# The modulation's partition sums as two-row products beside the attention, stored and turned once behind it

## What is computed

```
mod = jnp.dot(jax.nn.silu(cond), w_ada) + b_ada
sh1, sc1, gt1, sh2, sc2, gt2 = [m[:, None, :] for m in jnp.split(mod, 6, axis=-1)]
h = _rmsnorm(x, g_pre_mix) * (1 + sc1) + sh1
z = jnp.einsum('bld,de->ble', h, w_in)
...                                    # mLSTM over chunks in both directions, pooling mixer
x = x + gt1 * _rmsnorm(y, g_post_mix)
h2 = _rmsnorm(x, g_pre_ffn) * (1 + sc2) + sh2
...                                    # convolutional feed-forward
x = x + gt2 * _rmsnorm(f, g_post_ffn)
```

## Time and profile before

| | us |
|---|---|
| median of 3 runs (lowest, highest) | 1732.97 (1732.83, 1733.44) |
| the profiled execution's own time | 1731.54 |
| its span in the trace | 1729.7 |
| busy: PE | 1716.1 |
| busy: DVE | 1265.7 |
| busy: ACT | 703.4 |
| busy: POOL | 256.4 |

### The profile page before, as it was taken

The page is one execution under the profiler, slowest core; times in us unless marked ns, Lnnn a source line. Parts: engine busy times, 40 slices in busy tenths (PEclk is TensorE's granted clock), DMA queues, the critical chain, the costliest instruction groups (busy, mean ns, idle before and its releaser), DMA issues.

```text
span 1729.7 us, 27434 instructions
## 1 busy us (share of the span) xinstructions
PE 1716.1 (99%) x10568; PEld 1621.7 (94%) x10568; DVE 1265.7 (73%) x2754; ACT 703.4 (41%) x1300; POOL 256.4 (15%) x255
## 2 busy tenths in 40 slices
PE   8999999999999999999999999999999999999998
PEld 3999999999999999999988899999999999888887
DVE  4777677677677777573465589888888888788998
ACT  4543222343234243461244454433344334444454
POOL 1010000100100100010000061444333333100000
PEclk9999999999999999999999999999999999999999
DMA  9214333443344455364242331333322222686876
GB/s 347 68 44 148 86 116 113 124 116 124 106 129 148 121 154 169 136 228 147 74 139 91 111 103 66 111 105 104 105 76 67 71 70 69 215 277 218 273 249 245
DMA packets 216279, 236.21 MB, mean 137 GB/s; under 512 B 11568, under 2 KB 160828, under 8 KB 216148
## 3 DMA queue, kind: packets, MB, share of 16 engines
q1 hardware_dynamic: 200916, 179.54, 34.3%
q0 software_dynamic: 10752, 38.00, 6.4%
q10 hardware_dynamic: 4480, 16.91, 2.4%
HBM read 181.49 MB, written 52.92 MB: 136 GB/s over the span
## 4 chain that ended last, share of the span: by engine, by line
PE 93%; DVE 3%; DMA 1%; ACT 1%; SPq 1%; issue 0%; POOL 0%; ACTq 0%; DVEq 0%; POOLq 0%
PE ps L1470 23%; PE ps L1105 13%; PE ps L1107 12%; PE ps L1106 12%; PE ps L1412 6%; PE ps L1487 5%; PE ps L1488 5%; PE ps L1489 5%; PE ps L1277 2%; PE ps L1293 2%; PE ps L1294 1%; PE ps L1295 1%; PE ps L1134 1%; PE ps L1128 1%; DMA adaw<-in_w_ada_dram 1%; PE ps L1220 1%
## 5 line engine op out<-in xcount | busy, mean ns | idle before, releaser
L1105 PE MATMUL ps<-H_hi,ring_hi 128*128 128x384 f32 x1200 | 406.1, 338 | 0.4
L1107 PE MATMUL ps<-H_hi,ring_lo 128*128 128x384 f32 x1200 | 401.8, 335 | 0.0
L1106 PE MATMUL ps<-H_lo,ring_hi 128*128 128x384 f32 x1200 | 401.8, 335 | 0.0
L1105 PEld LDWEIGHTS ps<-H_hi,ring_hi 128*128 128x128 f32 x1200 | 225.6, 188 | 1.9 <-DVE H_lo L2208 1.6
L1106 PEld LDWEIGHTS ps<-H_lo,ring_hi 128*128 128x128 f32 x1200 | 225.6, 188 | 0.2
L1107 PEld LDWEIGHTS ps<-H_hi,ring_lo 128*128 128x128 f32 x1200 | 225.4, 188 | 0.0
L1470 PE MATMUL ps<-T_hi,up_hi 128*128 128x288 f32 x608 | 130.7, 297 | 0.3 <-ACT held_g L2043 0.3
L1470 PE MATMUL ps<-T_lo,up_hi 128*128 128x288 f32 x608 | 130.4, 296 | 0.0
L1470 PE MATMUL ps<-T_hi,up_lo 128*128 128x288 f32 x608 | 130.3, 296 | 0.0
L2208 DVE TENSOR_TENSOR up_lo<-up_raw,up_hi 128x512 fp32r<-128x512 f32 x114 | 88.4, 778 | 57.2 <-ACT up_hi L2001 57.2
L2441 DVE SCALAR_TENSOR_TENSOR ada_part<-raw,condT,ada_part 128x128 f32<-128x128 f32 x448 | 120.3, 346 | 0.0
(11 more groups left out here) (347 smaller groups left out, 3765.9 us busy)
## 6 DMA issues: line engine op xcount, KB each, us to landing
raw<-in_w_in_dram SPq DMA_DIRECT2D x44, 512.0 KB, 4.1
up_raw<-in_w_up_dram SPq DMA_DIRECT2D x38, 512.0 KB, 5.3
w_raw<-in_w_down_dram SPq DMA_DIRECT2D x66, 256.0 KB, 3.3
raw<-in_w_ada_dram SPq DMA_DIRECT2D x32, 512.0 KB, 5.1
X<-z_f SPq DMA_DIRECT2D x44, 256.0 KB, 4.0
GE<-z_gates SPq DMA_DIRECT2D x72, 128.0 KB, 3.8
w_sub<-in_w_down_dram SPq DMA_DIRECT2D x33, 256.0 KB, 3.9
z_w_diff<-w_raw SPq DMA_DIRECT2D x22, 256.0 KB, 2.5
```

Of the source, the lines that this page charges most:

```text
L1105: pe.matmul(out, whi, xhi, start=first, stop=False)
L1106: pe.matmul(out, whi, xlo, start=False, stop=False)
L1107: return pe.matmul(out, wlo, xhi, start=False, stop=last)
```

## The change

The sums 17 to 47 are made in another way and in another place; sum 16 stays as it was.

- DVE: behind the 16 products it copies `ada_part` (both conditionings, 128x256) into a high part, `part_hi`, and writes the rest as `part_lo`, which lies in the same memory as `ada_part`. Both are linked, that is each waits until the instruction before it is done.
- PE: `ada_sum` no longer stands ahead of the unit's blocks, but between block 0 and block 1. It is two matmuls with a stationary operand of two columns of ones (`ones_pair`), moving `part_hi` and then `part_lo` (256 columns), into bank 2. Ahead of it PE waits until bank 2 has been evacuated, and ahead of block 2 until ACT has evacuated block 0.
- ACT: it copies the row of 256 sums to `mod_row` (one partition), evacuates block 0, and issues a DMA of that row to `z_mod` ahead of the exponentials.
- DVE: `mod_row` lies in the memory of `kw_lo`, so ahead of the first kw tile it waits until the row is stored (`mod_rows_stored`). `part_hi` lies in the second half of a tile of `SC` that ACT now fills only by half in step 1.
- Behind the attention POOL loads the 62 rows, PE turns them once (step d == 2), and DVE adds the bias for all of them at once and forms the coefficients in step d == 4 (`second_coef`) instead of ahead of step 0.
- In unit 8 DVE does `pool_group` ahead of the products and no longer behind them.

What is moved and added on PE and on DVE stands in the listings of the order, and of those parts the diff below shows only a line or two.

```diff
+    part_hi = place("part_hi", [P, 2, P], F32R, at=base[0] - 2048 * SEEN + 1024)
     ada_part = place("ada_part", [P, 2, P])
+    part_lo = place("part_lo", [P, 2, P], F32R, at=base[0] - 1024)
+    mod_row = place("mod_row", [1, 2 * P], at=base[0] - 1024)     # behind kw_lo
...
             def ada_sum(a):
                 pe.wait_ge(ada_summed, a - ADA0 + 1)
-                for cond in range(2):
-                    mm = pe.matmul(ps[:, 0, 400 + cond:401 + cond], ada_part[:, cond, :], ones[:, :], start=True, stop=True)
+                if a == ADA0:
+                    for cond in range(2):
+                        mm = pe.matmul(ps[:, 0, 400 + cond:401 + cond], ada_part[:, cond, :], ones[:, :], start=True, stop=True)
+                else:
+                    for n, part in enumerate((part_hi, part_lo)):
+                        mm = pe.matmul(ps[0:2, 2, 0:2 * P], ones_pair[:, :], part[:, :, :].rearrange("p c n -> p (c n)"),
+                                       start=(n == 0), stop=(n == 1))
                 mm.then_inc(ada_used, 1)
...
                 for b in range(NB):
                     take0(q0 + b)
+                    if b == 2 and m > RU and m in ADA_AT:
+                        pe.wait_ge(evac0, q0 + 1)
...
+                    if b == 0 and m > RU and m in ADA_AT:
+                        take0(q0 + 2)
+                        ada_sum(ADA_AT[m])
...
+                if d == 2:
+                    pe.wait_ge(mod_rows_in, 16)
+                    pe.transpose(ps[:, 6, P:P + 2 * ROWS], mod_rows[:, :], ident[0:2 * ROWS, 0:2 * ROWS]).then_inc(rows_turned, 1)
...
+                    else:
+                        if rows_by(m) > 1:
+                            act.wait_ge(mod_rows_stored, 16 * (rows_by(m) - 1))
+                        act.activation(mod_row[:, :], ps[0:1, 2, 0:2 * P], ACT.Copy)
...
+                    if m > RU and m in ADA_AT:
+                        act.wait_ge(evac0, q0 + 1)
+                        act.dma_start(z_mod[rows_by(m) - 1:rows_by(m), :], mod_row[:, :]).then_inc(mod_rows_stored, 16)
...
+                if i < NT - 1 and rows_by(SEG + e):
+                    dve.wait_ge(mod_rows_stored, 16 * rows_by(SEG + e))
...
+                                link(ins)
+                                link(dve.tensor_copy(part_hi[:, :, :], ada_part[:, :, :]))
+                                sub_hi(part_lo[:, :, :], ada_part[:, :, :], part_hi[:, :, :]).then_inc(ada_summed, 1)
```

More of the change, by code:

```diff
@@ L142, in build, with rows_by @@
             ADA_AT[s] = ADA0 + len(ADA_AT)
+    ROWS = 48 - ADA0 - 1
+    def rows_by(m):
+        return sum(1 for s, a in ADA_AT.items() if s <= m and a > ADA0)
     raw_items = []
@@ L398, in build @@
     z_rows = nc.dram_tensor("z_rows", (2, 2, DM), F32, kind="Internal").ap()
+    z_mod = nc.dram_tensor("z_mod", (ROWS, 2 * P), F32, kind="Internal").ap()
     x1_dram = nc.dram_tensor("z_x1", (NT, P, DM), F32, kind="Internal").ap()
@@ L1321, in _ @@
                 take0(q0)
-                if m in ADA_AT:
-                    ada_sum(ADA_AT[m])
+                if m == RU:
+                    ada_sum(ADA0)
                 pe.wait_ge(lo_ready, m + 2 if kind == "v" and idx % 2 == 0 else m + 1)
@@ L1884, in _ @@
                     act.wait_ge(att_weights, seg + 1)
-                    act.activation(SC[:, seg % NT - 1, :, :], ps[:, 3, :].rearrange("p (a b) -> p a b", b=P),
+                    parts = 2 if seg % NT == 1 else 4
+                    act.activation(SC[:, seg % NT - 1, 0:parts, :], ps[:, 3, 0:parts * P].rearrange("p (a b) -> p a b", b=P),
                                    ACT.Copy).then_inc(att_cached, 1)
@@ L2229, in rows @@
                 return vT[:, col:col + n].unsqueeze(2).to_broadcast([P, n, 2])
+            dve.wait_ge(pool_seq, 7)
+            dve.tensor_copy(ones_pair[:, :], ones[:, :].to_broadcast([P, 2]))
             dve.wait_ge(small_in, 16 * 7)
@@ L2443, in ada_products @@
                         if k == KD - 1 and cond:
-                            ins.then_inc(ada_summed, 1)
+                            if a == ADA0:
+                                ins.then_inc(ada_summed, 1)
+                            else:
+                                link(ins)
+                                link(dve.tensor_copy(part_hi[:, :, :], ada_part[:, :, :]))
+                                sub_hi(part_lo[:, :, :], ada_part[:, :, :], part_hi[:, :, :]).then_inc(ada_summed, 1)
                         else:
@@ L2537, in _, with second_coef @@
                         head_scale(NORM_AT[m])
-            dve.wait_ge(evac0, 3 * use_of[("main", NM - 1)] + 3)
-            dve.scalar_tensor_tensor(out=coefA2[:, :, :], in0=modT[:, 32:40, :], scalar=1.0, in1=rows(V_GPF, KD),
-                                     op0=ALU.add, op1=ALU.mult)
-            for n, (mod, gain) in enumerate(((16, V_GQM), (40, V_GQF))):
-                ins = dve.tensor_tensor(coefG[:, n, :, :].rearrange("p c k -> p k c"), modT[:, mod:mod + KD, :], rows(gain, KD), ALU.mult)
-            ins.then_inc(coef2, 1)
+            def second_coef():
+                dve.wait_ge(rows_turned, 2)
+                at = ADA0 + 1
+                link(dve.tensor_tensor(modT[:, at:48, :], ps[:, 6, P:P + 2 * ROWS].rearrange("p (a c) -> p a c", c=2),
+                                       rows(V_BADA + at, ROWS), ALU.add))
+                dve.scalar_tensor_tensor(out=coefA2[:, :, :], in0=modT[:, 32:40, :], scalar=1.0, in1=rows(V_GPF, KD),
+                                         op0=ALU.add, op1=ALU.mult)
+                for n, (mod, gain) in enumerate(((16, V_GQM), (40, V_GQF))):
+                    ins = dve.tensor_tensor(coefG[:, n, :, :].rearrange("p c k -> p k c"), modT[:, mod:mod + KD, :],
+                                            rows(gain, KD), ALU.mult)
+                ins.then_inc(coef2, 1)
             for d in range(KD):
+                if d == 4:
+                    second_coef()
                 k = HEAD_ORDER[d]
```

31 lines of the change are left out of this document (18 added, 13 removed).

## The result

The changed kernel takes 1810.43 us (median of 4 runs, 1806.07 to 1812.34); the kernel before took 1733.2 us beside it (4 runs, 1732.83 to 1734.85). The ratio is 1.0435, 95% interval 1.0423 to 1.0448: slower by 4.35%. The forecast was 1771, range 1756 to 1787. The direction was right and the size was not: the time went up by 77 us where 38 were forecast, and it lies outside the range. The profiled execution of the changed kernel took 1809.66 us with a span of 1807.8 us, 78.1 us longer than the span before.

A forecast was written before the change was run, and what follows sets the result against it. PE was taken to bound the kernel. Unit terms 20.6 + 14.9 + 3.1 + 0.9 - 1.4 = +38.1 us took the profiled 1731.54 to about 1769.7, the median to 1771; range 1756 to 1787.

The forecast's parts named there:

- the 2.0 us of cover: In step 7, head 0, DVE ends v_lo 2.01 us before PE needs it; delay ahead of v_lo is free up to that.
- Sum to products: From the sum's start on PE behind block 0 until DVE can start the next products: 0.44 us.
- The copies: DVE's added copy and subtraction for part_hi and part_lo, with the wait for the last product: 0.76 us, bounds 0.6 to 0.95.
- the restart: PE starting again after waiting for DVE's v_lo, with a slower first matmul: about 0.17 us a stall, bounds 0 to 0.3.
- plain unit: One of 12 units in steps 2 to 7 without turns or gaps: +1.72 us each, 20.6 us in all.
- turn unit: One of 5 units with a sum and one more DVE instruction over 1152 columns: +2.97 us each, 14.9 us.
- covered units: Seven units with a sum where PE would not wait: each gains 0.2 us, -1.4 us in all.
- the smallest transfer listed lands after 3.1 us: Landing time taken for the stored row, so that it is there before DVE reaches kw at 11.9 us into the unit.
- rival 4: PE's clock falls during the new waits; one block at 1.2 GHz after each of 24 stalls, 100 us: 1870. Chance 4%.
- the one stall that I read: PE's idle time of 1.49 us ahead of 46.46 us, where the slice around it still showed the full clock.
- the short bounds: Lower bounds for release, copies and restart: 0.47 us less over 24 stalls, 11 us, giving 1760.
- Rival 3: The row's store lands late, after 7.3 us, so kw waits in 20 units: +20 us, 1791. Chance 8%.

## Why the prediction was wrong, and where it was right

**Right: what bounds the kernel, and the 2.0 us of cover.** PE is the bound, and DVE's idle time behind v_lo gave no cover. The version with the sum 1.0 us into block 0 stays inside the 2.0 and has no stall; the changed kernel, 2.8 us late and with the copies on top, stalls in 24 units, as counted.

**Right: the sizes in a unit.** Block 0 was to be 4.16 and took 4.17. Sum to products was to be 0.44 and took 297.01 - 296.50 = 0.51. The copies were to be 0.76: products to ring_lo now take 301.87 - 297.01 = 4.86 where they took 4.07, so 0.79. From block 0's start to the attention products the forecast said 14.65, and it is 306.98 - 292.33 = 14.65. That the two agree to the hundredth is luck: the sum to the products is 0.07 longer, the copies 0.03 and the block 0.01, while the restart costs 0.05 to this mark and not 0.17. Its slow first matmul falls behind the mark, and adds its 0.1 to the period. The period of a plain unit grew by 1.84 us (forecast 1.72), of a turn unit without a clock fall by 3.2 (2.97), of step 8 by 0.79 (0.69), of step 0 of the last head by 1.18 (1.0), of an odd value unit without the store's wait by 0.29 (0.3). The covered units gained 0.12 and not 0.20. Together 40.3 to 41.8 us where the sum said 38.1. PE's stalls were 1.75 to 1.81 and 3.08 to 3.13 us (1.9 and 3.2).

On the copies, the page "VectorE: DVE Perf Modes" of the Trainium skill (section "The DRAIN you can't avoid") would have taken off 0.10 a sum. The copy starts at 301.20, 0.04 behind the end of the last product (297.40 + 3.76) and some 0.39 behind that product's start, while products come every 0.26: the overlap was lost as forecast. No run here separates what the semaphore itself costs from the overlap that goes with it; the two together cost the 0.1.

**Wrong: "the smallest transfer listed lands after 3.1 us".** This step took the landing of a 64 KB transfer, the smallest that it listed, for all units and made the late landing a rival with a chance of 8%, thought of as 20 units and 7.3 us. It was four units and 7.8 to 10.3 us, worse than the upper bound, because POOL's stores of the state's last column are in the queues there. The other units' rows landed in 1.1 to 3.0 us. The mistake was to take one duration for a transfer without asking, unit by unit, what else is in flight. The stores were in the trace of before, once a head, and smaller than the smallest that the forecast read: 0.5 KB, landing after 10.1 us in the row of before shown with the result. Nor was 7.3 us the slowest kind: loads of 1024 KB took 13.1 us in that trace. A look at the DMA issues beside step 1 would have shown the stores. Price: 15.9 us of stalls where 3 were forecast, 13.1 us, and the clock falls behind the longer stalls.

**Wrong: rival 4's chance and its form.** It was given 4% and the price of "one block at 1.2 GHz behind each of 24 stalls", 100 us. Since the one stall that I read, 1.49 us, kept the full clock, I put the clock at nothing in the sum. The runs show a price between: 9 of 24 stalls are followed by a fall, and a fall takes 1.4 to 3.0 us, 19.8 us in all. The row used as evidence was one execution and a lucky one: the same stall was followed by a fall in six of the twelve traces. It was also shorter than the stalls that were forecast, 1.9 and 3.2 us. One execution of a stall shorter than those it is to bear out bounds nothing. The page "TensorE: Matmul & The Clock Gate" of the Trainium skill (section "HAM oscillation — how this bites in real kernels") was the better witness: by it waits that recur between bursts of work bring the array back to half rate. The traces agree in kind, with a fall behind 33 of 36 stalls of 3.08 us or more; the waits of the page's own example are as long as those or longer, and it gives no price for stalls of 1.8 us, of which 11 of 47 lost the clock. The traces do not show every stall doing so, which the 100 us of the rival had assumed.

**Wrong by omission: the start.** The new order in unit 8 was in the diff and got no price. It cost 1.4 us of waiting and, in the changed kernel, 1.7 us of clock.

**The range.** 1756 to 1787 held the bounds of the sum and part of one rival. Its inner ends were loosely added: the short bounds give 1771 - 11 = 1760 and the long ones 1771 + 12 = 1783, where the forecast has 1757 and 1784; the result lies outside either way. Rival 3 (1791) and a part of rival 4 came together: 1771 + 2 to 4 (terms of the sum) + 13 (store) + 20 (clock) + 4 (start) is the measured 1810 to about a microsecond. I had taken the rivals as exclusive, and they add up; worse, the one (longer stalls) feeds the other.

## What to carry to other kernels

When a dependence moves, compare the delay with the cover in the one unit where both can be read; that sum was right to 10%. Then price what the new stalls trigger: each stall that the bound engine gets beyond what it has stood so far may cost its clock as well, and a small transfer can land late where small stores of other queues are in flight. And read a stall's clock from more than one execution before you call it free. If the product of the move is wanted, put it as late as the cover allows and not one block later: the same sums cost 4.35% behind block 0 and gained 0.16% six matmuls into it.

## What the runs showed that I had not expected

- PE's granted clock fell to the lower level behind idle stretches as short as 1.75 us in an otherwise full timeline: 1.4 us into the work that followed in the stretch shown, but already inside the stall in six of the changed kernel's nine falls. Of equal stalls of 1.75 to 1.81 us in the attention steps 11 of 47 were followed by a fall; each cost 1.4 to 3.1 us. Near 47 us a stall of 1.47 to 1.49 us was followed by a fall in six of twelve traces, so that one execution at full clock does not show a stall to be free.
- Matmuls that nobody reads, in the place of stalls, made the kernel 19.5 us faster (1790.9 against 1810.4).
- Two stores of 0.5 KB in elements of 4 bytes took 7.0 to 11.9 us to land beside 128 KB stores, and with them held back a 1 KB store of another queue from 1.1 to 3.0 us to 7.8 to 10.3 us. Without them the kernel was 19.9 us faster; without the 128 KB stores beside them, 12.0 us.
- A pair of matmuls with a first operand of two columns and 256 moving ones took 0.23 us, no more than with 128 columns.
